# Dense products of a two-model transformer kernel: raw fp32 operands in two 64-column tiles instead of three products of rounded high and low halves

## What is computed

```
layer 0:  h += moba_and_dilated_attention(rms(h) @ w_in_ab) @ w_out_ab
layer 1:  h += nsa_attention(rms(h) @ w_in_nsa, compressed keys and values) @ w_out_nsa
both:     h += (silu(rms(h) @ w_gate) * (rms(h) @ w_up)) @ w_down          # 1024 x 2816
          h += sigmoid(rms(h) @ w_ple_gate) * (p @ w_ple_proj)
layer 2, 3: h += [rms(windowed_attention), rms(gated_short_conv)] @ w_out_2  # from rms(h) @ w_in_2
            h += hierarchical_moe(rms(h))      # 32 experts of width 512, top 2 of one group of 8
out = rms(h)
```

## Time and profile before

| | |
|---|---|
| median of three runs | 1897.4 us (1894.85 to 1900.9) |
| profiled execution, span from the first to the last instruction | 1897.5 us |
| TensorE matmul busy | 1822.5 us, 96% |
| VectorE busy | 861.8 us, 45% |
| ScalarE busy | 765.6 us, 40% |
| mean granted TensorE clock | 0.987 of full |
| bytes moved by DMA | 549.4 MB, 290 GB/s in the mean |

### The profile page before, as it was taken

The page is one execution under the profiler, slowest core; times in us unless marked ns, Lnnn a source line. Parts: engine busy times, 40 slices in busy tenths (PEclk is TensorE's granted clock), DMA queues, the critical chain, the costliest instruction groups (busy, mean ns, idle before and its releaser), DMA issues.

```text
span 1897.5 us, 27293 instructions
## 1 busy us (share of the span) xinstructions
PE 1822.5 (96%) x10299; PEld 1179.9 (62%) x10299; DVE 861.8 (45%) x1611; ACT 765.6 (40%) x1392; POOL 105.0 (6%) x146
## 2 busy tenths in 40 slices
PE   8999999998999999999999999999999999999997
PEld 6779998886799988974334333335975333433334
DVE  4766656678765566873112111114784111211113
ACT  5554334556543335532333333334542333333333
POOL 3420000112100000010000000000010000000000
PEclk9999999998999999999999999999998999999999
DMA  9545555551355554449999999998557999999995
GB/s 318 201 161 185 193 179 177 166 180 55 110 189 179 181 184 149 162 195 374 419 427 427 427 429 428 429 428 336 186 211 276 411 427 428 427 428 426 428 428 217
DMA packets 130593, 549.40 MB, mean 290 GB/s; under 512 B 8030, under 2 KB 67768, under 8 KB 103480
## 3 DMA queue, kind: packets, MB, share of 16 engines
q1 hardware_dynamic: 127080, 539.53, 72.3%
q0 software_dynamic: 3088, 8.10, 1.3%
q10 hardware_dynamic: 320, 0.34, 0.1%
HBM read 546.83 MB, written 1.11 MB: 289 GB/s over the span
## 4 chain that ended last, share of the span: by engine, by line
PE 75%; DMA 17%; DVE 5%; ACT 1%; POOL 1%; issue 1%; SPq 0%; POOLq 0%; DVEq 0%; ACTq 0%
PE pb L1350 28%; DMA raw<-in_w_expert_down 16%; PE pb L1912 14%; PE pb L1941 11%; PE pb L1645 6%; PE pb L1920 2%; PE pb L1930 2%; PE pb L1479 1%; PE pb L1456 1%; PE pb L1502 1%; PE pb L1579 1%; DVE parts L2104 1%; POOL rms L893 1%; PE pb L1362 1%; PE pb L1858 1%
## 5 line engine op out<-in xcount | busy, mean ns | idle before, releaser
L2104 DVE TENSOR_TENSOR parts<-raw,parts 128x2048 fp32r<-128x2048 f32 (+1 forms) x138 | 307.2, 2232 | 109.3 <-ACT parts L913 106.3
L913 ACT ACTIVATE parts<-raw 128x2048 fp32r<-128x2048 f32 (+1 forms) x138 | 256.6, 1867 | 210.9 <-PE pb L1350 154.4
L1912 PE MATMUL pb<-raw,xw 128*64 128x512 f32 x1360 | 323.9, 608 | 10.9 <-DMA raw<-in_w_expert_gate 10.9
L1350 PE MATMUL pb<-xT,parts 128*128 128x256 f32 (+1 forms) x2712 | 333.3, 283 | 0.0
L1350 PEld LDWEIGHTS pb<-xT,parts 128*128 128x128 f32 (+1 forms) x2712 | 329.2, 191 | 4.7 <-issue 2.9
L2720 DVE TENSOR_TENSOR qk<-qk,pb 128x256 f32<-128x256 f32 x126 | 53.1, 422 | 550.0 <-ACT qk L1205 549.8
L1350 PE MATMUL pb<-parts,xT 128*128 128x512 f32 (+1 forms) x1200 | 273.4, 386 | 2.7 <-DVE xT L2115 1.5
L1350 PEld LDWEIGHTS pb<-parts,xT 128*128 128x128 f32 x1200 | 218.8, 190 | 49.2 <-issue 4.0
L1912 PEld LDWEIGHTS pb<-raw,xw 128*64 128x64 f32 x1360 | 87.5, 138 | 156.4 <-issue 133.3
L1941 PE MATMUL pb<-raw,qk 128*64 128x512 f32 x624 | 142.8, 596 | 20.3 <-DMA raw<-in_w_expert_down 20.2
L1200 ACT ACTIVATE qk<-pb 128x512 f32<-128x512 f32 x126 | 74.9, 595 | 195.4 <-PE pb L1912 195.4
(11 more groups left out here) (338 smaller groups left out, 1692.9 us busy)
## 6 DMA issues: line engine op xcount, KB each, us to landing
raw<-in_w_expert_gate SPq DMA_DIRECT2D x41, 2048.0 KB, 10.0
raw<-in_w_expert_up SPq DMA_DIRECT2D x37, 2048.0 KB, 10.4
raw<-in_w_expert_down SPq DMA_DIRECT2D x35, 2048.0 KB, 10.7
spare<-in_w_expert_down SPq DMA_DIRECT2D x16, 2048.0 KB, 15.1
spare<-in_w_expert_up SPq DMA_DIRECT2D x14, 2048.0 KB, 13.4
raw<-in_w_ffn_gate SPq DMA_DIRECT2D x22, 1024.0 KB, 5.2
raw<-in_w_ffn_up SPq DMA_DIRECT2D x22, 1024.0 KB, 5.1
raw<-in_w_ffn_down SPq DMA_DIRECT2D x22, 1024.0 KB, 4.9
```

Source lines behind the costliest of these rows:

```text
L913: nc.scalar.activation(parts[:, (SPL0[seg] + k) % SPL, 0, 0:kk * nn], raw[:, place, 0:kk * nn], ACT.Copy).then_inc(hi_done[seg], 1)
L1350: ins = mm(out_ap, b if flip else a, a if flip else b, start=first and n == 0, stop=last and n == 2)
L1912: ins = mm(pb[m][rows, :], xw[:, 4 * hf + k, :], w[:, k, :], start=(hf == 0 and k < 2), stop=(hf == 1 and k >= 2))
L2104: v.tensor_tensor(two[:, 1, :], raw[:, place, 0:kk * nn], two[:, 0, :].bitcast(F32), ALU.subtract)\
```

## The change

- `three` becomes `two`: two fp32 matmuls, on the stationary columns 0 to 63 and 64 to 127, into the PSUM partitions 0 to 63 and 64 to 127, with the same moving operand. It takes the raw weight piece and one fp32 copy of the activations. All dense products use it: projections, convolution, output projections, feed-forward, `ple`, `p_proj`, router, compression, both gathers and the sum of the experts' results.
- Both `split_to` are gone, with `parts`, `hi_done`, `lo_done` and every call of them. TensorE waits for a piece's DMA (`landed_piece`); a place is loaded again when TensorE has used it.
- `raw` has twelve places in one ring. `plan` uses six of them as its `raw` and six as its `spare` places; with the three of `extra` these are fifteen places as before, and `first_wait` names other events for their first use.
- `evac_half`: ScalarE takes the blocks 0 and 1 of each half, VectorE the blocks 2 and 3, once each.
- The low halves of hidden values, attention outputs, windows, router weights, tokens and results are gone, with their instructions. The 48-column projection of layer 1 uses the common path and needs no transpose afterwards. The compression takes the weights as the stationary operand and windows and position as one moving operand of 120 columns; its selection products are gone.

```diff
-            def three(out_ap, x, w, k, kw, xcols, wcols, first, last, flip=False):
-
-                for n, (i, j) in enumerate(((0, 0), (1, 0), (0, 1))):
-                    a, b = x[:, i, k, xcols], w[j][:, kw, wcols]
-                    ins = mm(out_ap, b if flip else a, a if flip else b, start=first and n == 0, stop=last and n == 2)
+            def two(out_ap, stationary, moving, first, last):
+
+                for rows in (slice(0, HD), slice(HD, P)):
+                    ins = mm(out_ap[rows, :], stationary[:, rows], moving, start=first, stop=last)
                 return ins
+
+            def landed_piece(seg, s):
+
+                pe.wait_ge(arrived[seg][stream[seg][s][2]], stream[seg][s][3])
+                return piece_of(seg, s)
...
-                            ins = three(ffn_bank(kind, q, j), xT, both(0, s), k, k, slice(0, S),
-                                        slice(P * j, P * (j + 1)), k == 0, k == KC - 1, flip=True)
+                            ins = two(ffn_bank(kind, q, j), w[:, k, P * j:P * (j + 1)], xT[:, k, :], k == 0, k == KC - 1)
...
             def load(seg, i):
                 dst, src, place, _, _ = stream[seg][i]
-                if i >= RAW:
-                    sp.wait_ge(lo_done[seg], i - RAW + 1)
+                if i >= RING:
+                    sp.wait_ge(used[seg], i - RING + 1)
...
-                for c in range(4 * half, 4 * half + 4):
-                    dve.wait_ge(xT_a, tp_chunks(m) + c // 2 * 2 + 2)
+                for c in (4 * half + 2, 4 * half + 3):
+                    dve.wait_ge(tp_ready, tp_turned(m) + c // 2 + 1)
                     src = turn_bank(n, c)[:, S * (c % 2):S * (c % 2 + 1)]
-                    hi = xT[:, 0, c, :].bitcast(F32)
                     col = G_NORM[n]
-                    v.scalar_tensor_tensor(xT[:, 1, c, :], src, gT[:, col + c:col + c + 1], hi, ALU.mult, ALU.subtract)\
-                        .then_inc(xT_v, 1)
+                    v.tensor_scalar(xT[:, c, :], src, gT[:, col + c:col + c + 1], None, ALU.mult).then_inc(xT_v, 1)
...
-                    for i in range(2):
-                        ins = mm(pb[2 * half + t][:], selT[:, sc, P * t:P * (t + 1)],
-                                 y_slots(half)[:, i, 512 * sc:512 * (sc + 1)], start=(sc == 0 and i == 0),
-                                 stop=(sc == 3 and i == 1))
+                    ins = two(pb[2 * half + t][:], selT[:, sc, P * t:P * (t + 1)], y_slots(half)[:, sc, :], sc == 0, sc == 3)
...
                         for t in range(NT):
-                            for i in range(2):
-                                ins = mm(gather_bank(k)[:, 0:NS - EARLY], tokens(i, t, k), sel[:, t, EARLY:NS],
-                                         start=(t == 0 and i == 0), stop=(t == 1 and i == 1))
+                            ins = two(gather_bank(k)[:, 0:NS - EARLY], tokens(t, k), sel[:, t, EARLY:NS], t == 0, t == 1)
```

More of the change, by code:

```diff
@@ L323, in add, with piece_of @@
             return i
-        def both(seg, s):
-            k, n = stream[seg][s][4]
-            return [parts[:, (SPL0[seg] + s) % SPL, i, 0:k * n].rearrange("p (k n) -> p k n", k=k) for i in range(2)]
-        SPL0 = [0, 0, 0, 0]
+        def piece_of(seg, s):
+            return stream[seg][s][0]
         PJ = []
@@ L407, in put @@
                             waits = [w for w in waits if w[0] is not there_sem] + [(there_sem, at_least)]
-                    homes[job, i + n] = (buffer[:, x + n, :], there[x], 16 * count[x])
+                    homes[job, i + n] = (buffer[:, at_place + n, :], there, 16 * count[c])
                     rank[p] = use_of(job, i + n)
-                units.append((job, i, len(where), buffer[:, x:x + len(where), :], there[x], waits))
+                units.append((job, i, len(where), buffer[:, at_place:at_place + len(where), :], there, waits))
             order = [(0, 0), (0, 2), (1, 0), (1, 2), (0, 4), (1, 4)]
@@ L427, in plan @@
                     put(job, i + 1, single[1:])
-            return units, homes, raw_loads
+            return units, homes, raw_loads, [rank["spare", x] for x in range(RING - RAW)]
         PLAN = []
@@ L510, in build, with on_act, on_dve @@
               ("norm", 6), ("attn2", 0), ("norm", 7), ("norm", 8), ("attn2", 1), ("norm", 9)]
-        TPN = [8 if kind != "attn2" else 4 for kind, _ in TP]
-        def tp_chunks(m):
-            return sum(TPN[:m])
+        ON_ACT = {"norm": 4, "attn": 8, "attn2": 0}
+        ON_DVE = {"norm": 4, "attn": 0, "attn2": 4}
+        def on_act(m):
+            return sum(ON_ACT[kind] for kind, _ in TP[:m])
+        def on_dve(m):
+            return sum(ON_DVE[kind] for kind, _ in TP[:m])
         def tp_turned(m):
@@ L1642, in product @@
                 def product(q, j, t, c):
-                    w = both(0, down[q - 1])
-                    for n, (i, p) in enumerate(((0, 0), (1, 0), (0, 1))):
-                        ins = mm(pb[2 * c + t][:], hidT[:, j, i, P * t:P * (t + 1)],
-                                 w[p][:, j, 512 * c:512 * (c + 1)], start=(q == 1 and j == 0 and n == 0),
-                                 stop=(q == NQ and j == 1 and n == 2))
-                    return ins
+                    w = piece_of(0, down[q - 1])
+                    return two(pb[2 * c + t][:], hidT[:, j, P * t:P * (t + 1)], w[:, j, 512 * c:512 * (c + 1)],
+                               q == 1 and j == 0, q == NQ and j == 1)
                 wait_half(n_in)
@@ L1665, in ffn @@
                     pe.wait_ge(hT_done, NQ * f + q)
[L1666 removed]
+                    landed_piece(0, down[q - 1])
                     if q < NQ:
@@ L1806, in moe @@
                     for k in range(k0, k0 + 4):
-                        for i in range(2):
-                            ins = mm(pb[t][:, 0:2 * (NEG + NE)], xT[:, i, k, P * t:P * (t + 1)],
-                                     wrs[:, k, :, :].rearrange("p i n -> p (i n)"), start=(k == 0 and i == 0),
-                                     stop=(k == KC - 1 and i == 1))
+                        ins = two(pb[t][:, 0:NEG + NE], xT[:, k, P * t:P * (t + 1)], wr[:, l, k, :], k == 0, k == KC - 1)
                 ins.then_inc(rt_ready, 1)
@@ L2288, in attention @@
                         turned_probs(layer, i - 2)
-                    if i >= 4 and z[i - 4].last:
-                        pair_lo(layer, i - 4)
-                    if i == n:
-                        split_to(0, OPW[layer][0][1] + 1)
             def boundary(n, add):
-                seg, first = NEXT[n]
                 for c in range(2):
```

547 lines of the change are left out of this document (179 added, 368 removed).

## The result

The changed kernel takes 2070.9 us (median of 4 runs, 2066.0 to 2073.0), the kernel before 1897.8 us beside it: a ratio of 1.091 (95% interval 1.089 to 1.093). It is slower by 173 us; the forecast said 185 us slower, 2083 us, with 2055 to 2105 as the likeliest case's range.

The account below looks back on a forecast made before the run. Dense stages bound by TensorE, expert stages first by TensorE, then by transfers awaiting routing. 103.0 + 65.0 - 2 + 12.9 + 8.4 - 3 + 9 - 4 - 4 = +185 us on 1897.5: 2083 us, likeliest range 2055 to 2105.

Parts of the forecast that it names:

- The frame: Dense stages are bound by TensorE's instruction stream: its added work is paid in full, vector engines' savings only in visible waits.
- The prices of the products: Dense products: 592 of 512 columns at 0.858 against 0.684 us, +103.0; 928 of 256 at 0.430 against 0.360, +65.0.
- The rival of a dearer 256-column pair: Dense 256-column products cost 0.51 us each as stationary loads may not hide: +74 us, 2156 us; chance 0.09.
- The attention fill: 32 512-column products between attention steps no longer pay for changing to the full array: -2 us, bounds 0 and 4.
- Selections: Gathers and sum of experts' results as fp32 products: +12.9 us for the sum, +8.4 for the later gather, 0 for the earlier.
- The result sum: Sum of the experts' results after the last job: 64 instructions, 14.6 us, become 32 products, 27.5 us: +12.9 us.
- The late gather: 384-column gather between jobs 0 and 1: 12.2 us busy becomes 20.6, +8.4 us counted in full, bounds 0 and 8.4.
- the early gather: 128-column gather: 64 instructions, 13.2 us busy, become 32 products, 6.9 us at full clock; counted 0, bounds -6 and +3.
- the forecast's clock term: Around the routing the clock may fall for some microseconds in other places than before: 0, bounds -5 and +5.
- Changes of kind: Transposes and other full-array products among tiled ones: 30 islands at 0.3 us, +9 us, bounds 2 and 15.
- Compression: Compression's 32 + 32 instructions and selection products, about 10 us, become 32 products of 120 columns, 7 us: -3 us.
- What goes: Dropped splits give back 4 of 5.8 us of TensorE waits; earlier `xT` at start, boundaries and routing gives -4 us.

Follow-up runs that it names:

- the opposite case: Kernel before with one fp32r product (high halves alone) instead of three for the 256-column products of gate, up and gated convolution: 1812.2 us, ratio 0.955.
- the untiled kernel: Changed kernel with one 128-column fp32 matmul in place of each pair of 64-column tiles: 2069.7 us, ratio 1.091.
- the mixed kernel: Kernel before, splits kept, with fp32 pairs on the high halves for the 896 dense 256-column products alone: 1969.3 us, ratio 1.038.

## Why the prediction was right

**The frame.** TensorE bounds the dense stages, so what it gains is paid in full and what the vector engines lose is worth little. Shown by busy +179.6 and idle -9.0 us in the kernel after, by 2.4 to 3.7 us for nearly all split work, and by the opposite case, where less TensorE work did bring time until the loop behind it closed.

**The prices of the products** (+103.0, +65.0): right. 6.87 and 13.81 us for the blocks; 37.7 us more for each feed-forward part. The rival of a dearer 256-column pair (2156 us) is gone with 13.81 / 32 = 0.43 us. Ratios of 1.25 at 512 columns and 1.19 at 256 came out. The four passes that the Trainium skill gives for true fp32 (FP8 and Floating Point Precision, TensorE Precision Notes), against three reduced products, led the forecast to an estimate of about 2160 us; the measured 2070.9 us don't bear out a ratio of 4/3.

**The attention fill** (-2): the busy time of the group behind the fill products went from 25.3 to 24.1 us at the same shape, and that of a smaller one of 96 beside it from 10.0 to 9.5. Right in kind; in size as far as busy times show it.

**Selections.** The result sum has 64 + 64 records of 512 columns, which are 32 products, and their mean of 595 to 597 ns is that of the dense ones: 32 x 0.858 = 27.5 us, as forecast. The late gather: 5.16 us for 32 records, four such shares in all, 20.6 us, as forecast; what it replaced was 11.8 us by pace (2.9 to 3.0 us for 16 instructions), not the 12.2 of busy time that the sum took. The forecast counted it in full, against a bound by which the transfers would hide it, and that is right: the stretches from the first expert product to the result sum grew by 2.2 and 1.2 us, although the first expert products in them, as follows, became 1.9 and 2.6 us shorter. But the cost is partly given back on either side. Before, the first expert job's products, 32 records, took 8.81 and 9.48 us in the two layers; now they take 6.87, which is the full-clock price. The windows of the two traces over the early gather and the products behind it, first the kernel before, then after:

```profile
851.00:857.98 6.98, 6.89 (x34) 6.78 (x36) 3.05 (x5) 0.00 (x0) 0.00 (x0) 0.52 0.74 272
857.98:866.80 8.82, 8.82 (x34) 2.66 (x33) 7.00 (x13) 0.60 (x1) 0.00 (x0) 0.80 0.78 284
```

```profile
993.50:999.50 6.00, 6.00 (x66) 5.97 (x68) 0.92 (x3) 0.00 (x0) 0.00 (x0) 0.61 0.69 243
999.50:1006.40 6.90, 6.90 (x34) 2.25 (x32) 6.61 (x13) 0.60 (x1) 0.00 (x0) 1.00 0.98 357
```

The granted clock was 0.52 in the early gather and 0.80 behind it; now it is 0.61 and 1.00. In layer 3 it was 0.58 and 0.74 and is 0.68 and 1.00. The clock comes back before the expert products instead of among them. That is -1.9 and -2.6 us at the products, -4.5 where the forecast's clock term was 0 with bounds of 5 either way. The early gather has a term of its own, 0 with bounds of -6 and +3, and became 0.9 us shorter in each layer (6.89 and 6.26 before, 6.00 and 5.38 after). Together it is about -6. What makes the clock come back earlier wasn't tested.

**Changes of kind** (+9): the step that was mis-sized. The change out of and into tiles exists: eight transposes in a boundary take 1.02 us in the chain above, 0.79 before (130.24 - 129.45 in the old timeline), 0.87 in the untiled kernel. The tiles alone so cost 0.15 us, and the rest of the 0.23 is there without tiles too. The Trainium skill, TensorEngine Tiling (Array Packing), Key Properties, says that a change of tiling mode drains TensorE; the 0.15 us agree with that. But only 14 blocks of eight and some smaller ones pay it, at 0.23 us and not 0.3, some 4 us; and without any tiles the total is the same (2069.7 against 2070.9 us, less than the runs' spread). The 0.15 us read from one expert job was right; doubling it for the way in, and counting 30 islands, was not.

**Compression** (-3): from `compress_turn`'s block (402.12 and 479.60) to the heads behind (428.47 and 504.57) it is 26.35 us before and 24.97 after, -1.4 us. Sixteen dense products of 512 columns lie in it and add 16 x 0.174 = 2.8, so the compression and the 48-column projection beside it gave 4.2. **What goes** (-4, -4): 9 us less idle TensorE against 8 forecast. VectorE's busy time fell by 371 us and not only by the 307 named as a sign, since the low halves of the activations went too; the forecast gave neither a price. Here too the sum is surer than its parts: L1645's wait of 3.1 us became 0.5, L1350's 2.7 became nothing, and the boundaries' fell from 4.9 to 3.8 us.

**The sum.** 185 forecast, 170.6 in the span. Idle: -9 against -8. Busy: 179.6 against 193.3 (185 and the 8 us of idle). Of the 13.7 us too much, some 6 are the clock and the early gather at the start of the expert stages, 5 the changes of kind and 1 the compression; what is left, some 2, is less than the runs of one kernel differ. This split is an estimate from blocks of two traces; no run took one of these terms out by itself but the untiled one. All of it lies in the forecast's own range, and no rival's mechanism showed.

## What to carry to other kernels

In this kernel a full fp32 product cost 1.25 times three fp32r products (0.858 against 0.684 us at 512 columns), so dropping a split can pay only where the vector engines, not TensorE, end the stage: ask first which of them idles. Where TensorE is shortened, find the loop that its work had covered (free a place, split, make the operand, multiply) and add that up before counting the gain; two thirds of the work taken out of gate, up and the gated convolution (215 us) brought 85 us. And a wait of TensorE can cost more than its length, as the granted clock fell to 0.50 behind a wait of 2.34 us here, so useful work put in its place can be free.

## What was not expected of the hardware

- Two 64-column fp32 tiles that share one moving operand run wholly at once, and gain nothing over one 128-column matmul: 394.3 and 394.2 us for the same 896 products. One tile alone takes as long as both, 20.68 us a quarter.
- A small difference in a repeated short wait decided on the clock. With waits of 2.34 us in each 13.5 us TensorE ran 3.4 us of every quarter at 1.2 GHz (0.50 granted); with waits of 1.35 us in each 11.2 us it stayed at 2.4 GHz. Where between these it turns wasn't tried.
- Changing between fp32 pairs and full-array fp32r products cost about 0.17 us each time (0.35 us for the two of a quarter), and it shows in the blocks' start-to-start times, hardly in the mean length of an instruction (380 ns in the mixed kernel, 379 without the changes).
